# Two-layer mixture-of-experts encoder on one core: expert outputs added to the residual rows in DRAM

## The chip, the core and the metric

The kernel runs on one core of one Trainium2 chip. The metric is the device time of a run in microseconds; the kernel before takes 2674.23 us (median of 3 runs, 2671.6 to 2676.23). A core has TensorE (PE), VectorE (DVE), ScalarE (ACT), GpSimd (POOL) and SyncE (SP, which issues most transfers). They run beside each other and are ordered by semaphores only. Transfers issued by any of them run on the same 16 DMA engines. The profile is of one execution.

## What is computed

The input x is 1024 tokens of 1024 floats (f32). There are two layers, each a token mixer and then a mixture of experts (MoE), each with a norm before it and added to x:

```python
for i in range(2):
    if i == 0:
        x = x + short_conv_mixer(rms_norm(x, w), conv_w_in, conv_k, conv_w_out)
    else:
        x = x + mla_mixer(rms_norm(x, w), ...)        # latents 384+256+64, 8 heads, full softmax
    x = x + hier_moe(rms_norm(x, ffn_w), ...)

def hier_moe(h):                                      # 64 experts in 8 groups of 8
    g_sel = argmax(h @ w_group + b_group)             # one group per token
    e_top = top2(expert logits of that group + bias)  # two experts in it
    gate  = g_prob[g_sel] * e_prob[e_top] / sum(e_prob[e_top])
    out[token] += gate * ((silu(h @ w_gate[e]) * (h @ w_up[e])) @ w_down[e])   # w: 1024x384, 384x1024
```

Every expert's weights (4.7 MB) are read once per layer, 302 MB a layer. A token has two choices, so there are 2048 rows of 1024 floats of expert output in a layer.

## The kernel before

`build_trunk` runs four phases, one block each with a barrier of all engines behind it: `conv_phase` (mixer of layer 0 and its output projection), `moe_phase` of layer 0, `attention_phase` (latents, attention, output projection), `moe_phase` of layer 1. x lives in SBUF (`c.x`, 8 tiles of 128 tokens) throughout.

**Output projection** (`OutProjection`, L446 to L593, in both mixers). Per tile of tokens TensorE multiplies, VectorE adds to x (L538), ScalarE and GpSimd make the norm, and SP stores the normed rows to `h_rows` in DRAM (`sp_store_rows`, L471). The routing of two tiles at a time runs on VectorE (`dve_route`). At its end SP starts the first weights of the experts: gate and up weights have 4 slots, down weights 4 slots; two of the down slots lie in the arena, one in `c.turned` and its neighbours and one in a spare piece of the arena (L425 to L430).

**Expert layer** (`moe_phase`, L1025). VectorE ranks the choices of each expert (64 rows a round, one round here in each layer) and compares the ranks with columns (`find_ranks`, L1267, a one-hot of 128 x 2048); TensorE multiplies this with coded token numbers (`index_products`, L1392) into a table of DRAM row numbers, `gather_idx`, and VectorE makes `scatter_idx` beside it (L1346, L1347). A row of 1024 floats is handled as two half rows on 128 partitions. Then, for each expert, in an order written out by hand:

- GpSimd copies one column of the table (L1159), issues an indirect gather of the normed rows (L1162), later copies a column of the other table (L1169) and issues an indirect scatter of the outputs (L1172). Between them `complete` waits until the scatter of the expert before has landed, so at most one scatter is in flight.
- TensorE turns the gathered rows (L1410), multiplies gate and up (L1420), turns the products (L1430) and multiplies down (L1439). The order in one step is `gate_and_up(g)`, `turn_x(g+1)`, `down(g-1)`, `turn_h(g)`. After the first expert's `gate_and_up` and the second's `turn_x` it also does `index_products(r + 1)`.
- ScalarE copies products (L1210), makes SiLU (L1216) and copies the output (L1221). VectorE scales the turned rows (L1324) and multiplies (L1333).
- SP waits for each slot to be used and loads the next weights into it, the gate and up weights of expert g+4 after those of g, then the down weights, in that fixed order.

The scatters write to `y_rows`, 2 x 1024 rows: a row for the first choice of a token and one for the second, without the gates. Every row is written once.

**After the experts**, VectorE makes the gates (`make_gates`, L1297). In layer 0, VectorE and ScalarE split the weights of the latent projection, and SP loads pairs of rows from `y_rows` (L1010, six in this block, two later); in `attention_phase` VectorE adds both rows times their gates to each x tile (`combine`, L1813, two instructions a tile) before TensorE may turn it (L2001) and ScalarE may square it. In layer 1, SP loads the pairs (L1140), ScalarE scales the first row (L1247), VectorE adds the second and x (L1372, L1375), and SP stores x to the output (L1143).

**Attention**: 64 tiles (8 heads x 8 tiles of queries). TensorE makes 128 x 1024 scores in two halves of 512 (L2058, L2060), VectorE finds the row maximum of all 1024 (L1931) and minus the scaled maximum (L1934), ScalarE takes the exponential (L1743).

## Time and profile before

| | |
|---|---|
| median of 3 runs | 2674.23 us (2671.6 to 2676.23) |
| the profiled execution: device time | 2678.26 us |
| its span, first to last instruction | 2676.5 us |
| mean granted TensorE clock | 0.938 of full |
| PE / PEld / DVE / ACT / POOL busy | 87% / 55% / 30% / 24% / 25% |
| DRAM read / written | 687.59 MB / 46.14 MB |
| weight queue (q1) / GpSimd's queue (q0) | 666.65 MB / 33.64 MB |

The phases in the span: convolution mixer and projection from 0 to 412 us, experts of layer 0 to 1174 (their weights start at 399), latents to 1300, attention to 1759, projection to 1880, experts of layer 1 to 2642 (their weights start at 1867), the sum of pairs and the stores to the end. A busy share over the whole span mixes these. TensorE shows 87% although in the expert layers it is waiting for weights again and again; its granted clock there changes between its two levels.

### The profile page before, as it was taken

To read this page: it belongs to the slowest core of one execution; us is meant where nothing else is said; L and a number is where in the kernel's file an instruction comes from. 1 tells how busy PE (TensorE), PEld (TensorE's weight loads), DVE (VectorE), ACT (ScalarE), POOL (GpSimd) and SP (SyncE) were. 2 spreads that over 40 slices of the span, in tenths; PEclk is the share of its full clock that TensorE was granted. 3 is DMA by queue.
4 is the path that set the end of the run, shared out by engine and by line. 5 is a ranking of instruction groups with operands and counts; after the bars stand their busy time and mean duration, and the time that the engine had idled before them with its cause. 6 is when DMAs were issued, how large, how long until landed. Compare 5 with 4: busy or idle time off the path is not lost. (4 is left out here: it accounts for less than half of the span.)

```text
span 2676.5 us, 35898 instructions
## 1 busy us (share of the span) xinstructions
PE 2321.1 (87%) x12316; PEld 1463.0 (55%) x12318; DVE 809.3 (30%) x2022; ACT 636.9 (24%) x1360; POOL 679.6 (25%) x1092
## 2 busy tenths in 40 slices
PE   8999995988888888878799999999598888888883
PEld 6888782433333333348688898768243333333331
DVE  4322443100000000045578777644310000000003
ACT  4000221111110111134366666642011111111111
POOL 3222211212222212211655555211122122122120
PEclk9999997999999999989899999999799999999997
DMA  5111219999999999980000000101999999999997
GB/s 133 48 47 31 79 45 397 422 424 423 424 423 424 424 424 424 423 328 1 9 9 9 18 10 1 64 24 63 396 422 424 423 424 424 424 423 424 424 423 300
DMA packets 136774, 701.39 MB, mean 262 GB/s; under 512 B 36192, under 2 KB 65888, under 8 KB 87536
## 3 DMA queue, kind: packets, MB, share of 16 engines
q1 hardware_dynamic: 116208, 666.65, 60.7%
q0 software_dynamic: 20480, 33.64, 3.3%
q8 instruction: 49, 0.80, 0.1%
q14 instruction: 37, 0.30, 0.0%
HBM read 687.59 MB, written 46.14 MB: 274 GB/s over the span
## 5 line engine op out<-in xcount | busy, mean ns | idle before, releaser
L1420 PE MATMUL ps<-arena 128*64 128x384 f32 x2048 | 389.8, 539 | 90.1 <-DMA arena<-in_exp_w_up 88.0
L1420 PE MATMUL ps<-gate_up,arena 128*64 128x384 f32 x2048 | 384.9, 533 | 92.5 <-issue 92.5
L1324 DVE TENSOR_TENSOR arena<-ps,xw 128x512 f32<-128x512 f32 x128 | 88.6, 692 | 957.1 <-PE ps L1410 957.1
L1420 PEld LDWEIGHTS ps<-gate_up,arena 128*64 128x64 f32 x2048 | 181.3, 149 | 264.8 <-issue 183.9
L1420 PEld LDWEIGHTS ps<-arena 128*64 128x64 f32 x2048 | 158.5, 150 | 290.5 <-issue 242.2
L1210 ACT ACTIVATE arena<-ps 128x384 f32<-128x384 f32 x128 | 62.9, 491 | 898.7 <-PE ps L1420 898.7
L943 PE MATMUL ps<-hT_split,w_split 128*128 128x512 f32 x1152 | 265.6, 392 | 7.3 <-DVE hT_split L837 7.3
L1439 PE MATMUL ps<-arena 128*64 128x512 f32 x1152 | 268.3, 600 | 0.0
L1169 POOL COPY col_idx<-scatter_idx 128x1 int32 (+1 forms) x128 | 23.4, 183 | 920.2 <-ACT arena L1221 899.4
L943 PEld LDWEIGHTS ps<-hT_split,w_split 128*128 128x128 f32 x1152 | 217.3, 189 | 53.1 <-DVE hT_split L837 8.0
L1221 ACT ACTIVATE arena<-ps 128x512 f32<-128x512 f32 x128 | 76.4, 597 | 372.9 <-PE ps L1439 364.1
L1162 POOL DMA_INDIRECT arena<-h_rows,col_idx x128 | 135.2, 1057 | 114.6 <-POOL col_idx L1159 93.0
L1333 DVE TENSOR_TENSOR arena<-arena,ps 128x192 f32<-128x192 f32 x128 | 45.4, 354 | 387.7 <-ACT arena L1216 387.7
L1172 POOL DMA_INDIRECT y_rows<-arena,col_idx x128 | 132.0, 1031 | 112.8 <-POOL col_idx L1169 112.8
L1439 PEld LDWEIGHTS ps<-arena 128*64 128x64 f32 x1152 | 74.7, 136 | 121.4 <-issue 109.6
L1410 PEld LDWEIGHTS ps<-ident,arena 128*128 128x128 f32 x512 | 71.8, 209 | 101.8 <-issue 101.8
L2058 PE MATMUL ps<-k_split,q_split 128*128 128x512 f32 x384 | 115.0, 408 | 5.8 <-DVE k_split L1926 5.8
L1410 PE MATMUL ps<-ident,arena 128*128 128x128 f32 x512 | 96.5, 311 | 26.1 <-DMA arena<-h_rows,col_idx 26.1
L2082 PE MATMUL ps<-probsT,v_split 128*128 128x256 f32 x768 | 108.7, 292 | 5.6 <-DVE probsT L1940 5.6
L1430 PEld LDWEIGHTS ps<-ident,arena 128*128 128x128 f32 x384 | 53.6, 199 | 103.1 <-issue 102.2
L2082 PEld LDWEIGHTS ps<-probsT,v_split 128*128 128x128 f32 x768 | 101.4, 193 | 10.4 <-issue 6.6
L742 POOL TENSOR_TENSOR w_split<-arena,w_split 128x1024 fp32r<-128x1024 f32 x24 | 57.4, 2391 | 182.5 <-ACT w_split L779 182.5
(236 smaller groups left out, 3221.5 us busy)
## 6 DMA issues: line engine op xcount, KB each, us to landing
arena<-in_exp_w_down SPq DMA_DIRECT2D x96, 1536.0 KB, 28.6
arena<-in_exp_w_gate SPq DMA_DIRECT2D x64, 1536.0 KB
arena<-in_exp_w_up SPq DMA_DIRECT2D x64, 1536.0 KB
gate_up<-in_exp_w_gate SPq DMA_DIRECT2D x64, 1536.0 KB
gate_up<-in_exp_w_up SPq DMA_DIRECT2D x64, 1536.0 KB
down<-in_exp_w_down SPq DMA_DIRECT2D x32, 1536.0 KB, 28.6
arena<-in_conv_w_in SPq DMA_DIRECT2D x24, 512.0 KB, 3.8
arena<-y_rows SPq DMA_DIRECT2D x12, 1024.0 KB, 8.5
```

Of the source, the lines that this page charges most:

```text
L742: pool.tensor_tensor(w_split[:, j, LOW, :, :], w_raw[:, slot, :, :], w_split[:, j, HIGH, :, :], ALU.subtract).then_inc(w_low_ready, 1)
L943: last = pe.matmul(c.ps[:, 3 * h + j, :], w_split[:, j, a, k, :], hT_split[:, b, k, h * BANK:(h + 1) * BANK], start=(k == 0 and a == b), s ...
L1162: pool.indirect_dma_start(gathered[:, slot, :], None, h_halves, bass.IndirectOffsetOnAxis(ap=col_idx[:, slot, :], axis=0), bounds_check=2 ...
L1172: pool.indirect_dma_start(y_halves, bass.IndirectOffsetOnAxis(ap=col_idx[:, 2 + slot, :], axis=0), y[:, slot, :], None, bounds_check=4 * S ...
L1210: act.activation(gate_up[:, slot, :], c.ps[:, 2 + slot, 0:FF], ACT.Copy).then_inc(gate_up_copied, 1)
L1221: act.activation(y[:, slot, :], c.ps[:, 6 + slot, :], ACT.Copy).then_inc(y_copied, 1)
L1324: dve.tensor_tensor(xT[:, slot, :, :, :].rearrange("p j h m -> p (j h) m"), c.ps[:, slot, :].rearrange("p (a m) -> p a m", m=RANKS), bc(c. ...
L1410: last_ = pe.transpose(c.ps[:, slot, j * P:(j + 1) * P], rows[:, j, :], c.ident[:, :])
L1420: last_ = pe.matmul(c.ps[row:row + RANKS, 2 + slot, 0:FF], xT[:, slot, j, half, :], w_gate_up[w_slot][:, i, (4 * half + j) * FF:(4 * half ...
L1439: last_ = pe.matmul(c.ps[half * RANKS:(half + 1) * RANKS, 6 + slot, :], hidden[:, slot, j, :], w_down[w_slot][:, j, half * BANK:(half + 1) ...
L2058: pe.matmul(out, q_split[:, a, 0, q], k_split[:, h % 2, 2 * b, keys], start=(n == 0), stop=False)
L2082: last = pe.matmul(c.ps[:, 7, 0:2 * P], v_split[:, a, (q // 4 * NT + kt) % V_RING, :], probsT[:, b, kt, :], start=(kt == 0 and a == b), st ...
```

## The change

- The DRAM tensor `y_rows` (2048 rows) is gone, and so are `scatter_idx` and the ring of pair buffers. New is `x_rows` (1024 rows). During each output projection SP also stores every x tile, in layer 0 to `x_rows` and in layer 1 to the output tensor, each ahead of the normed rows of that tile.
- The scatters have `compute_op=ALU.add`: they add to the rows of `x_rows` or of the output. They use the same row numbers as the gathers.
- The gates are made at the begin of a round in the expert layer, ahead of the first expert's `expert_x`; they are split in three bf16 parts, multiplied with the choice (`gate_coded`) and spread by 48 matmuls (`spread_gates`) to one column for each expert. ScalarE's copy of an expert's output takes that column as its scale. `find_ranks(r + 1)` moves behind these.
- After layer 0, SP loads 8 x tiles of 512 KB from `x_rows` into `c.x`, and TensorE and ScalarE wait for them directly. After layer 1, nothing follows the last scatter.
- The third down slot lies in x tiles 5 to 7, whose rows are in DRAM by then; the one-hot and the gate pieces lie in x tiles 0 to 3.
- In the attention, the row maximum is found in two halves, each after its own half of the scores, and one instruction takes the larger and scales it.

```diff
@@ ExpertWeights
-        self.down.append(c.arena[:, self.SPARE_AT:self.SPARE_AT + KF * D].rearrange("p (j d) -> p j d", d=D))
+        self.down.append(c.x[:, NT - KF:, :])
@@ OutProjection
+    def sp_begin_sums(self, sp, t):
+        sp.wait_ge(self.x_added, 2 * t + 2)
+        sp.dma_start(self.sum_rows[t * P:(t + 1) * P, :], self.c.x[:, t, :]).then_inc(self.sums_begun, 16)
     def sp_store_rows(self, sp):
         for t in range(NT - 1):
+            self.sp_begin_sums(sp, t)
             self.norm.sp_store(sp, t)
         sp.wait_ge(self.products, 2 * NT)
         self.experts.load_gate_up(sp, 0, 0)
+        self.sp_begin_sums(sp, NT - 1)
         self.norm.sp_store(sp, NT - 1)
...
+        sp.wait_ge(self.sums_begun, 16 * NT)
@@ LatentPlaces
-    def load_y(self, sp, t):
-        src = self.c.y_rows.rearrange("(k t p) d -> t p k d", k=2, p=P)[t]
-        sp.dma_start(self.y_pair[t % Y_RING], src).then_inc(self.y_loaded[t % Y_RING], 16)
+    def load_x(self, sp, t):
+        sp.dma_start(self.c.x[:, t, :], self.c.x_rows[t * P:(t + 1) * P, :]).then_inc(self.x_loaded[t], 16)
@@ moe_phase, SP
                 sp.wait_ge(y_stored, count * NE + AHEAD)
-                for t in range(Y_RING):
-                    places.load_y(sp, t)
-            else:
-                sp.wait_ge(y_stored, count * NE + AHEAD)
                 for t in range(NT):
...
-                sp.wait_ge(stored, 16 * NT)
+                    places.load_x(sp, t)
@@ moe_phase, GpSimd
-                pool.tensor_copy(col_idx[:, 2 + slot, :], scatter_idx[:, bass.ds(e, 1)]).then_inc(pool_step, 1)
+                pool.tensor_copy(col_idx[:, 2 + slot, :], gather_idx[:, bass.ds(e, 1)]).then_inc(pool_step, 1)
...
-                pool.indirect_dma_start(y_halves, bass.IndirectOffsetOnAxis(ap=col_idx[:, 2 + slot, :], axis=0),
-                                        y[:, slot, :], None,
-                                        bounds_check=4 * S - 1, oob_is_err=False).then_inc(scatter_done[slot], 16)
+                to_rows = bass.IndirectOffsetOnAxis(ap=col_idx[:, 2 + slot, :], axis=0)
+                pool.indirect_dma_start(sum_halves, to_rows, y[:, slot, :], None, compute_op=ALU.add,
+                                        bounds_check=2 * S - 1, oob_is_err=False).then_inc(scatter_done[slot], 16)
@@ moe_phase, ScalarE
-                act.activation(y[:, slot, :], c.ps[:, 6 + slot, :], ACT.Copy).then_inc(y_copied, 1)
+                act.activation(y[:, slot, :], c.ps[:, 6 + slot, :], ACT.Copy,
+                               scale=gate_cols[:, bass.ds(e, 1)]).then_inc(y_copied, 1)
@@ moe_phase, VectorE
+            def code_gates(chain):
+                rest = gates[:, :, :]
+                for part in range(GATE_PARTS - 1):
+                    chain.sync(dve.tensor_copy(rounded[:, part, :, :], rest))
+                    chain.sync(dve.tensor_copy(gate_parts[:, part, :, :], rounded[:, part, :, :]))
+                    left = gate_rest if part == 0 else gate_parts[:, GATE_PARTS - 1, :, :]
+                    chain.sync(dve.tensor_tensor(left, rest, gate_parts[:, part, :, :], ALU.subtract))
+                    rest = left
+                for k in range(2):
+                    coded_k = dve.tensor_tensor(gate_coded[:, k, :, :, :], bc(chosen[:, k, :, :], 2, GATE_PARTS),
+                                                bc(gate_parts[:, :, k, :].rearrange("p a t -> p t a"), 3, NE), ALU.mult)
+                coded_k.then_inc(gates_coded, 1)
...
-                find_ranks(r + 1)
-                g0 = r * NE
-                expert_x(g0, 0)
+                g0 = r * NE
+                make_gates(in_round)
+                code_gates(in_round)
+                expert_x(g0, 0)
+                dve.wait_ge(gate_products, r + 1)
+                dve.tensor_copy(gate_cols, c.ps[:, IDX_BANK, FF + NE:FF + 2 * NE]).then_inc(gate_cols_ready, 1)
+                find_ranks(r + 1)
...
-            make_gates()
@@ moe_phase, TensorE
+            def spread_gates(r):
+                pe.wait_ge(gates_coded, r + 1)
+                for n in range(2 * NT):
+                    for part in range(GATE_PARTS):
+                        last_ = pe.matmul(c.ps[:, IDX_BANK, FF + NE:FF + 2 * NE], onehot[:, n, :],
+                                          gate_coded[:, n // NT, n % NT, part, :], start=(n + part == 0),
+                                          stop=(n == 2 * NT - 1 and part == GATE_PARTS - 1))
+                last_.then_inc(gate_products, 1)
...
                 pe.wait_ge(gate_up_copied, g0 + free(1))
+                spread_gates(r)
                 index_products(r + 1)
@@ attention_phase, VectorE
-            def combine(t):
...
             def find_max(s):
                 slot = s % 2
-                dve.wait_ge(scores, s + 1)
-                dve.tensor_reduce(row_max[:, slot, :], c.ps[:, 2 * slot:2 * slot + 2, :].rearrange("p a b -> p (a b)"),
-                                  X, ALU.max).then_inc(max_found, 1)
-                dve.wait_ge(max_found, s + 1)
-                dve.tensor_scalar(minus_max[:, slot, :], row_max[:, slot, :], -SCALE, None,
-                                  ALU.mult).then_inc(bias_ready, 1)
+                for half in range(2):
+                    dve.wait_ge(scores, 2 * s + half + 1)
+                    dve.tensor_reduce(row_max[:, slot, half:half + 1], c.ps[:, 2 * slot + half, :],
+                                      X, ALU.max).then_inc(max_found, 1)
+                dve.wait_ge(max_found, 2 * s + 2)
+                dve.tensor_scalar(minus_max[:, slot, :], row_max[:, slot, 0:1], row_max[:, slot, 1:2], -SCALE,
+                                  ALU.max, ALU.mult).then_inc(bias_ready, 1)
@@ attention_phase, TensorE
             def turn_x(t):
-                pe.wait_ge(x_added, t + 1)
+                pe.wait_ge(places.x_loaded[t], 16)
```

## Rows read from the trace of the kernel before

**Rows 1.** Busy time by stretch: us, PE, PEld, DVE, ACT, POOL busy, clock, DMA share, GB/s.
```profile
560.00:1080.00 520.00, 445.64 (x2256) 197.19 (x2254) 46.04 (x88) 58.53 (x132) 109.50 (x177) 0.93 1.01 424
1300.00:1700.00 400.00, 387.51 (x2441) 348.39 (x2440) 313.77 (x917) 250.44 (x590) 207.92 (x403) 1.00 0.03 10
...
2674.00:2676.00 2.00, 0.00 (x0) 0.00 (x0) 0.00 (x0) 0.00 (x0) 0.00 (x0) 0.50 0.05 18
```

**Rows 2.** Chain of waits, layer 1: start us, us, what.
```profile
2036.03 5.38 PE ps L1420 x32
...
2045.91 37.10 DMA arena<-in_exp_w_up
```

**Rows 3.** Timeline, end of layer 1: start us, us, engine, line, operation [idle before].
```profile
2635.11 0.98 POOL L1172 DMA_INDIRECT y_rows<-arena,col_idx  x1 [0.86 <-POOL col_idx L1169]
...
2638.35 0.18 POOL L1169 COPY col_idx<-scatter_idx 128x1 int32<-128x1 int32 x1 [2.25 <-ACT arena L1221]
...
2639.39 0.98 POOL L1172 DMA_INDIRECT y_rows<-arena,col_idx  x1 [0.86 <-POOL col_idx L1169]
2641.79 12.05 SPq L1140 DMA_DIRECT2D arena<-y_rows  x8
```

**Rows 4.** The scatters of layer 0, by tile: durations in ns, first and last start.
```profile
L1172 POOL DMA_INDIRECT y_rows<-arena,col_idx x64: 984/1032/1493, 459.7 to 1171.4; - x64
...
DMA to landing us min/median/max: 2.6/7.3/8.4
```

**Rows 5.** Timeline, end of layer 0 and begin of the latents.
```profile
1171.09 6.99 DVE L1020 SCALAR_TENSOR_TENSOR w_lat_low<-arena,norm_w,w_lat_high 128x704 fp32r<-128x704 f32 x8 [0.32 <-ACT w_lat_high L1014]
...
1174.65 0.90 SPq L1010 DMA_DIRECT2D arena<-y_rows  x2
...
1176.80 1.01 SPq L1010 DMA_DIRECT2D rows<-y_rows  x2
1179.20 0.38 SPq L1624 DMA_DIRECT2D arena<-in_mla_w_q_up  x1
...
1182.28 1.97 PE L2001 MATMUL ps<-ident,x 128*128 128x128 f32 x8 [12.72 <-DVE x L1813]
```

**Rows 6.** Timeline, first and last of the 19 steps of the gates, layer 1.
```profile
2634.43 0.22 DVE L1257 TENSOR_TENSOR arena<-exps,picked 128x64 f32<-128x64 f32 x1
...
2638.59 0.17 DVE L1257 TENSOR_TENSOR gates<-arena 128x8 f32<-128x8 f32 x1
```

**Rows 7.** Timeline, begin of the experts of layer 1.
```profile
1893.09 2.29 DVE L1268 TENSOR_TENSOR onehot<-arena,rank_of_col 128x2048 bf16<-128x2048 f32 x1
1893.33 2.10 POOL L1159 COPY col_idx<-gather_idx 128x1 int32<-128x1 int32 x1 [10.28 <-DVE scatter_idx L1347]
...
1904.76 1.12 PE L1410 MATMUL ps<-ident,arena 128*128 128x128 f32 x4 [13.10 <-DMA arena<-h_rows,col_idx]
...
1915.08 1.10 PE L1396 MATMUL ps<-coded,onehot 128*128 128x64 bf16 x32
...
1916.50 0.61 PE L1430 MATMUL ps<-ident,arena 128*128 128x128 f32 x3 [0.33 <-ACT arena L1210]
...
1925.87 0.33 SPq L443 DMA_DIRECT2D arena<-in_exp_w_down  x1
```

**Rows 8.** Busy time by stretch, two microseconds at the begin of layer 1.
```profile
1924.00:1926.00 2.00, 2.00 (x12) 0.62 (x9) 0.00 (x0) 0.05 (x1) 0.00 (x0) 1.00 0.25 104
```

**Rows 9.** DMA queues from 560 to 1080 us: packets, MB, share; issues with their number.
```profile
q1 hardware_dynamic: 19125, 208.93, 95.3%
q0 software_dynamic: 7101, 11.35, 5.8%
...
arena<-h_rows,col_idx POOLq DMA_INDIRECT x45
```

**Rows 10.** GpSimd's waits from 560 to 1080 us: total us, times, longest.
```profile
POOL col_idx L1169 <- ACT arena L1221: 330.7, 44, 9.6
```

**Rows 11.** The maximum over all scores of a tile, by line: duration in ns, times.
```profile
L1931 DVE TENSOR_REDUCE turned<-ps x64: 1224/1225/1226, 1317.1 to 1747.2; 128x1 f32<-128x1024 f32 x64
```

More of the change, by code:

```diff
@@ L989, in __init__ @@
         self.low_ready = sems("w_lat_low_ready")
-        self.y_loaded = [sems(f"y_pair_loaded{i}") for i in range(Y_RING)]
+        self.x_loaded = [sems(f"x_sums_loaded{t}") for t in range(NT)]
         self.small_loaded = sems("latent_small_loaded")
@@ L1082, in moe_phase @@
     y_copied = sems("y_copied")
-    y_pair_loaded = [sems(f"y_pair_loaded{i}") for i in range(Y_RING)]
-    gates_ready = sems("gates_ready")
-    first_scaled = sems("first_scaled")
-    summed = sems("summed")
-    x_added = sems("x_added")
-    stored = sems("stored")
+    gates_coded = sems("gates_coded")
+    gate_products = sems("gate_products")
+    gate_cols_ready = sems("gate_cols_ready")
     def done(g):
@@ L1100, in moe_phase @@
     h_halves = c.h_rows.rearrange("t (h d) -> (t h) d", h=2)
-    y_halves = c.y_rows.rearrange("t (h d) -> (t h) d", h=2)
+    sum_halves = (c.out[0] if last else c.x_rows).rearrange("t (h d) -> (t h) d", h=2)
     def rounds(eng):
@@ L1242, in _ @@
                 return
-            act.wait_ge(gates_ready, 1)
-            for t in range(NT):
-                act.wait_ge(y_pair_loaded[t % Y_RING], 16 * (t // Y_RING + 1))
-                first = y_pair[:, t % Y_RING, 0, :]
-                act.activation(first, first, ACT.Copy, scale=gates[:, 0, t:t + 1]).then_inc(first_scaled, 1)
         @block.vector
@@ L1295, in _, with make_gates, tt, red @@
             dve.tensor_copy(n_rounds[:, :], t_[0][:, 1:2]).then_inc(rounds_ready, 1)
-            def make_gates():
+            def make_gates(chain):
+                def tt(out, a, b, op):
+                    chain.sync(dve.tensor_tensor(out, a, b, op))
+                def red(out, a, op):
+                    chain.sync(dve.tensor_reduce(out, a, X, op))
                 group, first, second = (c.picked[:, i, :, :] for i in range(3))
@@ L1306, in make_gates @@
                     red(t_[4], e, ALU.add)
-                    step.sync(dve.reciprocal(t_[5 + i], t_[4]))
+                    chain.sync(dve.reciprocal(t_[5 + i], t_[4]))
                 for i, total in enumerate((5, 6, 6)):
@@ L1310, in make_gates @@
                 tt(t_[10], t_[8], t_[9], ALU.add)
-                step.sync(dve.reciprocal(t_[11], t_[10]))
+                chain.sync(dve.reciprocal(t_[11], t_[10]))
                 for k in range(2):
@@ L1632, in _ @@
             load_router(sp, c, 1, router_loaded)
-            for t in range(Y_RING, NT):
-                sp.wait_ge(x_squares, t - Y_RING + 1)
-                places.load_y(sp, t)
             with sp.Fori(1, NH // 2) as pair:
@@ L1640, in _ @@
             sp.wait_ge(up_products, TILES)
-            sp.wait_ge(scores, TILES - NT)
+            sp.wait_ge(scores, 2 * (TILES - NT))
             out_projection.sp_load(sp)
@@ L1807, in sine_inputs @@
                 dve.tensor_scalar(turns_, turns_, PI_MAX, -PI_MAX, ALU.min, ALU.max).then_inc(sin_in, 1)
-            def combine(t):
-                dve.wait_ge(places.y_loaded[t % Y_RING], 16 * (t // Y_RING + 1))
-                for k in range(2):
-                    wait(dve, pair_added, t + 1 if k == 1 else 0)
-                    dve.scalar_tensor_tensor(out=c.x[:, t, :], in0=places.y_pair[t % Y_RING][:, k, :],
-                                             scalar=c.gates[:, k, t:t + 1], in1=c.x[:, t, :], op0=ALU.mult,
-                                             op1=ALU.add).then_inc((pair_added, x_added)[k], 1)
             def low_x(t):
@@ L2061, in score @@
                                          start=False, stop=(a == LOW))
-                last.then_inc(scores, 1)
+                    last.then_inc(scores, 1)
             def turn_probs(s, turned):
```

88 lines of the change are left out of this document (34 added, 54 removed).

## The prediction

> **What bounds the kernel now.** I read the 40 slices of the page first, then the busy time by stretch, the chain of waits, the DMA queues, and the timelines of the places that the diff touches. The two expert layers are bounded by the transfer of their weights: over 520 us in the first of them the DMA engines are full at 424 GB/s while VectorE, ScalarE and GpSimd are busy 46, 59 and 110 us [rows 1]. The chain of waits shows it too: one expert's products at 2036.03, then 37.1 us of waiting for weights until 2083.0, and so on [rows 2]. In these layers a microsecond of engine work costs nothing and a microsecond of transfer costs a microsecond. The attention stage is bounded by TensorE, busy 387.5 of 400 us with VectorE at 313.8 [rows 1].
>
> **Part 1, the end of layer 1: gain.** Now the last scatter starts at 2639.39 and has landed when SP issues the pair loads at 2641.79 [rows 3]. After that 8.4 MB of pairs are read and combined and 4.2 MB stored, until DMA's share falls to 0.05 in the stretch from 2674 to 2676 [rows 1]; the span ends at 2676.5. All of this goes: the output is complete when the last scatter has landed. The last transfer ends near 2674.2 (the small share in those 2 us is some 0.1 us, and a write receipt), so I keep 2.3 us from it to the end of the span; the end would be 2641.8 + 2.3 = 2644.1, a gain of 32.4 us. Against it: an adding scatter must read its destination before it writes, and the trace of before has no adding transfer. An unloaded scatter of before takes 2.4 us from its start to SP's next step [rows 3]; one more trip costs between 0 and another 2.4. I take 1.0, below the middle because the 2.4 hold 0.98 us of the issuing instruction. The scatter before the last starts at 2635.11 and would land at 2638.4, just as the last one's index copy starts anyway (2638.35) [rows 3]; with 2.4 more it would delay that by 1.5. Gain: 31.4 us (28.5 to 32.4).
>
> **Part 2, the end of layer 0.** Now SP issues six pair loads from 1174.65 to 1177.81, VectorE splits the weights until 1178.08, the stage's barrier lets SP begin the next stage at 1179.20, and two VectorE additions to the first tile hold TensorE until 1182.28 [rows 5]. From there the latent projection is one unbroken run of matmuls, so the later pairs and additions are hidden now and taking them out gives nothing: only the first start counts. In the changed kernel the last scatter lands 1.0 later, at 1175.65; SP issues eight loads at 0.53 us (3.16 us for six), until 1179.9; with the same 1.4 us to the barrier's end and 0.2 to the first transpose TensorE begins at 1181.5, its rows long there. The wait that takes the additions' place is SP's eight issues ahead of the barrier. Gain: 0.8 us (2.6 at best, a loss of 1.5 with 2.4 more in the landing).
>
> **Part 3, the begin of both expert layers: loss.** The gates, their three bf16 parts and two products with the choice move ahead of the first expert on VectorE. The 19 small steps of the gates take 4.33 us (2634.43 to 2638.76) [rows 6]; the 6 of the coding at the same 0.23 us make 1.4; the two products of 1,536 elements are priced from the 2,048-element comparison of 2.29 us [rows 7] at 1.7 each. Together 9.2 us, from 1893.1 to 1902.3. The cover is the first gather, whose rows are turned at 1904.76 to 1905.9 [rows 7]: this costs nothing, with 3.6 us to spare. What is moved too is that comparison (L1268). GpSimd's first index copy, 0.18 us elsewhere [rows 3], stood 2.10 us beside it and ended with it (1895.43 and 1895.38) [rows 7]. Without it the first gather starts up to 1.9 us earlier, I take 1.8, and with it the first expert; the spare is then 1.8 us.
>
> The Trainium skill says ("SBUF — State Buffer", section "Who interferes with whom") that a VectorE instruction with two SBUF inputs keeps GpSimd from reading SBUF while it runs. By that rule, the trace agrees with its 2.10 us, the gate steps that now stand there may hold the copy for one of them, 0.2 us, and no more.
>
> Behind the first expert's products TensorE now gets: 48 products that spread the gates (32 index products take 1.10 us from 1915.08 [rows 7], so 1.65, until 1916.73), then it waits for VectorE's copy (0.2, with the hand-over 0.4) and the comparison (2.29), until 1919.5; then the 32 index products, and the turn of the first hidden rows starts at 1920.8 instead of 1916.50 [rows 7]. That is 4.3 us later; the second expert's multiply, queued behind the comparison on VectorE, fits in. Net of the 1.8 it is 2.5 us. Nothing covers it: the DMA engines have by then filled every slot and stand at a share of 0.25 [rows 8] until the first down products release the next load at 1925.87 [rows 7], and transfer bounds the layer from there. So 5.0 us for both layers (0 if TensorE's wait is half as long, 9 if the early gather brings nothing). The x stores in each output projection (4.2 MB) run where DMA idles; the last of them (0.5 MB, 1.2 us), pushed in among the first weights, ends in the same hole: 0, or 1.2 each if the hole closes.
>
> **Part 4, the adding scatters in the transfer-bound stretch: the large loss.** In the same 520 us, 45 gathers and the scatters (44 by [rows 10]) took 5.8%, 30.2 us, or 0.339 us of all 16 engines each; the weight queue moved 208.93 MB in 95.3%, at 422 GB/s [rows 9]. The two queues fill the time together, so a scatter's bytes displace weights one for one. An adding scatter reads its source and its destination and writes once. The low end: the second read runs beside other writing and costs 0. The nearest row for the other end: a whole further scatter, 0.339 us. The 2,048 choices of a layer make 8.4 MB of rows; 123 of the 128 scatters lie in the bound stretches, 16.1 MB, and at the stream's 422 GB/s their second read takes 38.3 us (0.31 each; by 0.339 it is 41.7). I take 38.3, since gathers, scatters and loads share one budget in the rows whichever way they go.
>
> The Trainium skill ("Collectives: The Full Stack", section "The bandwidth ceiling: the fold count and why AG ≠ RS ≠ AR") puts a reduction inside the DMA engine at half a copy's rate, because it reads two sources and not because of the addition. By that rule the price is the one taken here; no run of this case shows it yet.
>
> Each scatter also waits on GpSimd for the earlier one to land, ahead of its index copy. Now GpSimd idles 330.7/44 = 7.5 us before that copy, and for ScalarE's result, not for the scatter [rows 10]; the median landing is 7.3 us [rows 4].
>
> **Part 5, attention.** The maximum of 1,024 elements takes 1.225 us, 64 times [rows 11]. Two halves cost about 0.16 us more and the first runs beside the second half's scores; but VectorE has 20% to spare and TensorE 3% [rows 1]. I take 1.0 us of gain from the last tiles, where TensorE waits a little (bounds: gain 4, loss 2).
>
> **Sum**, on the profiled execution's own 2678.3 us (span 2676.5): -31.4 - 0.8 + 5.0 + 38.3 - 1.0 = +10.1, so 2688.4. The median of the runs, 2674.2, is 4.1 lower; on it the forecast is 2684, slower by 0.4%. A measurement of this kernel tells about 0.2%, 5.3 us, from no change.
>
> **Rivals.**
> 1. The second read is hidden, the kernel is faster. The engines' writing side would be the bound, with reads from DRAM beside it. For it: no row separates the two sides. Against: DMA is as full whichever direction is under way. Part 4 falls to between 0 and 15 us; with 8, 2674.2 - 31.4 - 0.8 + 5.0 - 1.0 + 8 = 2654 (2646 to 2661).
> 2. The chain of scatters becomes the bound, the kernel is much slower. In layer 0 scatters start every 11.3 us (459.7 to 1171.4, 63 steps) [rows 4], 11.6 with part 4; copy and gap ahead of a start are 1.06 us [rows 3]. So it decides from a landing of 10.6 us. A loaded landing is 7.3, an unloaded 2.6 [rows 4]: if the queueing of 4.7 doubles with the second read, it is 12.0, the period 13.1, and 126 x (13.1 - 11.3) = 227 us replace part 4: 2873. For it: the queueing is there. Against: if only bytes are added, landing stays near 8.
> 3. The engine's addition is slow as well: 0.7 us a scatter instead of 0.31, 123 x 0.39 = 48 us more, 2732.
> 4. That the change doesn't do what it says, a result still stored at the end: the diff removes loads and stores there, so I give this nothing.
>
> **How the numbers follow.** The forecast 48% (its own range 2668 to 2702), rival 1 30%, rival 2 12%, rival 3 10%. The range, 2648 to 2735, leaves out the best end of rival 1 and nearly all of rival 2. Faster: rival 1 and the low end of the forecast's case, 0.32. Within 0.2%: 0.10. Slower: 0.58.
>
> **What would show it.** Four experts in the bound stretch take 47.1 us now (2083.1 less 2036.0 [rows 2]) and should take 48.3; at 47.1 rival 1 holds. The software queue's share should rise from 5.8% to about 8.5%. GpSimd should still wait for ScalarE before a scatter; if it waits for the landing, rival 2. DMA's hole behind the first four experts' weights should be 2.5 us longer in each layer, and the span should end some 5 us after the last scatter's start. I am wrong if four experts take the same time, or over 50 us.

## The result, and the profile after

The changed kernel takes 2682.8 us (median of 7 runs, 2678.8 to 2685.7) where the kernel before takes 2675.0 in runs beside it: 1.0027 times as long (1.0016 to 1.0039), slower by 0.3%. A second set of runs gave 1.0038 (1.0025 to 1.0052; its medians are 7.0 us apart). The forecast was 2684.

The profiled execution took 2681.45 us, its span is 2679.7, at a mean granted clock of 0.944. That is only 3.2 more than the profiled execution of before, which lay 3 us above its own median. The traces therefore show where 3.2 us come from; the other 4 to 5 between the medians lie in no single place that a trace shows.

The expert layers first. Busy time of the same stretches as [rows 1] and [rows 8], columns as there:

```profile
560.00:1080.00 520.00, 440.11 (x2238) 191.48 (x2236) 46.02 (x88) 61.59 (x132) 135.76 (x179) 0.94 1.02 414
1300.00:1700.00 400.00, 382.23 (x2394) 345.33 (x2395) 320.95 (x972) 243.39 (x584) 212.76 (x413) 0.99 0.03 10
```

The DMA engines are as full as before, and move 414 GB/s where it was 424. VectorE has 7 us more in the attention stage (the halves of the row maximum). The queues, issues and GpSimd's waits in that first stretch, against [rows 9] and [rows 10]:

```profile
q1 hardware_dynamic: 18664, 203.85, 92.5%
q0 software_dynamic: 9978, 11.59, 9.3%
...
x_rows<-arena,col_idx POOLq DMA_INDIRECT x45, 9.6
arena<-h_rows,col_idx POOLq DMA_INDIRECT x44, 9.5
```
```profile
POOL col_idx L1163 <- DMA x_rows<-arena,col_idx: 192.6, 30, 6.9
POOL col_idx L1163 <- ACT arena L1215: 117.6, 15, 8.6
```

GpSimd's queue is counted with about as many bytes as before (11.59 MB, where it was 11.35) and takes 9.3% of the engines instead of 5.8%. It has 2,877 packets more, some 64 for each of the 45 scatters: in the trace's packet records an adding scatter goes in packets of 2 KB, 176 ns each, where before gathers and scatters go in packets of 4 KB, 160 ns each. A read of the destination shows in no byte count. In 30 of 45 cases GpSimd waits for the landing of the scatter before, where it waited for ScalarE 44 times of 44. The scatters themselves, by tile, against [rows 4]: the issuing instruction takes 1.60 us instead of 1.03 and the landing, here over both layers, 9.6 instead of 7.3.

```profile
L1167 POOL DMA_INDIRECT x_rows<-arena,col_idx x64: 1566/1602/2202, 461.8 to 1192.3; - x64
```
```profile
DMA to landing us min/median/max: 3.7/9.6/10.5
```

The chain of waits in layer 1, against [rows 2]. Its early part runs from scatter to scatter. Its late part runs from weights to weights, four experts in 48.2 us (2486.74 to 2534.97) instead of 47.1:

```profile
2000.30 9.40 DMA out<-arena,col_idx
2010.12 0.17 POOL col_idx L1163
...
2486.74 5.38 PE ps L1427 x32
2496.63 38.22 DMA arena<-in_exp_w_up
2534.97 5.38 PE ps L1427 x32
```

The timeline at the end of layer 1, against [rows 3]. The index copy of the last scatter now waits 3.23 us for a landing, and the span ends at 2679.7, 8.4 us after the last scatter's start (37.1 before). Of these 8.4 us the landing takes 3.7:

```profile
2665.14 2.79 PE L1446 MATMUL ps<-down,arena 128*64 128x512 f32 x12 [1.15 <-DVE arena L1343]
...
2665.48 1.57 POOL L1167 DMA_INDIRECT out<-arena,col_idx  x1 [0.86 <-POOL col_idx L1163]
...
2670.28 0.18 POOL L1163 COPY col_idx<-gather_idx 128x1 int32<-128x1 int32 x1 [3.23 <-DMA out<-arena,col_idx]
2671.32 1.57 POOL L1167 DMA_INDIRECT out<-arena,col_idx  x1 [0.86 <-POOL col_idx L1163]
```

Most of the other 4.7 is a drain, GpSimd's last instruction of the block but for semaphores, from 2675.6 on. Its two executions (minimum, median and maximum in ns), one at the end of each expert layer, here and in the kernel whose scatters do not add (plain_scatter below):

```profile
L1112 POOLq DRAIN  x2: 2918/2987/3056, 1198.0 to 2675.6; - x2
```
```profile
L1112 POOLq DRAIN  x2: 1535/1604/1672, 1175.8 to 2636.0; - x2
```

The beginning of the experts of layer 0 (that of layer 1 has the same order), against [rows 7]:

```profile
445.30 1.56 PE L1403 MATMUL ps<-gate_coded,onehot 128*128 128x64 bf16 x48
...
446.90 0.22 DVE L1363 COPY x<-ps 128x64 f32<-128x64 f32 x1 [9.51 <-PE ps L1403]
447.04 2.28 DVE L1259 TENSOR_TENSOR onehot<-arena,rank_of_col 128x2048 bf16<-128x2048 f32 x1
...
449.38 1.11 PE L1394 MATMUL ps<-coded,onehot 128*128 128x64 bf16 x32 [2.52 <-DVE onehot L1259]
450.32 0.58 PE L1437 MATMUL ps<-ident,arena 128*128 128x128 f32 x3
...
459.66 0.33 SPq L442 DMA_DIRECT2D arena<-in_exp_w_down  x1
```

From the starts of such marks the span can be cut into pieces that add up. "Again" is a second profile of the same kernel, taken for the experiments.

| piece, us | before | after | changed by |
|---|---|---|---|
| begin to first scatter of layer 0 | 459.7 | 461.8 | +2.1 |
| first to last scatter of layer 0 | 711.7 | 730.5 (again 731.3) | +18.8 |
| last scatter to first turn of x | 10.9 | 10.5 | -0.4 |
| first turn to first score | 130.2 (again 128.5) | 126.2 (again 124.3) | -4.0 |
| first to last score | 433.8 | 430.7 (again 432.6) | -3.1 |
| to the barrier before layer 1 | 135.8 | 136.6 (again 134.3) | +0.8 |
| barrier to first scatter of layer 1 | 45.7 | 47.1 (again 47.7) | +1.4 |
| first to last scatter of layer 1 | 711.6 | 727.9 (again 728.6) | +16.3 |
| last scatter to the end | 37.1 | 8.4 (again 8.4) | -28.7 |
| sum | 2676.5 | 2679.7 | +3.2 |

### The profile page after: what moved, and what is told of

Its sections match the earlier page's. It is cut to its first block and busy times, and to the rows that moved or that the text cites. A ratio compares the mean times of both kernels' runs of the same rounds, so it can differ in the third digit from the quotient of the medians.

```text
span 2679.7 us, 36367 instructions
## 1 busy us (share of the span) xinstructions
PE 2321.2 (87%) x12412; PEld 1456.8 (54%) x12414; DVE 790.8 (30%) x2070; ACT 635.3 (24%) x1352; POOL 748.9 (28%) x1092
## 5 line engine op out<-in xcount | busy, mean ns | idle before, releaser
L1427 PE MATMUL ps<-arena 128*64 128x384 f32 x2048 | 380.8, 529 | 74.6 <-DMA arena<-in_exp_w_up 72.4
L1427 PEld LDWEIGHTS ps<-gate_up,arena 128*64 128x64 f32 x2048 | 173.0, 147 | 258.1 <-issue 199.6
L1427 PEld LDWEIGHTS ps<-arena 128*64 128x64 f32 x2048 | 154.8, 148 | 268.8 <-issue 223.3
L1163 POOL COPY col_idx<-gather_idx 128x1 int32 (+1 forms) x128 | 23.2, 181 | 888.1 <-ACT arena L1215 343.9
L1215 ACT ACTIVATE arena<-ps,x 128x512 f32<-128x512 f32 x128 | 88.0, 688 | 456.8 <-PE ps L1446 453.8
L1446 PE MATMUL ps<-arena 128*64 128x512 f32 x768 | 188.6, 628 | 0.0
L1167 POOL DMA_INDIRECT x_rows<-arena,col_idx x64 | 103.1, 1610 | 56.2 <-POOL col_idx L1163 56.2
L1167 POOL DMA_INDIRECT out<-arena,col_idx x64 | 102.5, 1602 | 57.8 <-POOL col_idx L1163 57.8
```

Source lines behind the costliest of these rows:

```text
L1167: pool.indirect_dma_start(sum_halves, to_rows, y[:, slot, :], None, compute_op=ALU.add, bounds_check=2 * S - 1, oob_is_err=False).then_inc ...
L1215: act.activation(y[:, slot, :], c.ps[:, 6 + slot, :], ACT.Copy, scale=gate_cols[:, bass.ds(e, 1)]).then_inc(y_copied, 1)
L1427: last_ = pe.matmul(c.ps[row:row + RANKS, 2 + slot, 0:FF], xT[:, slot, j, half, :], w_gate_up[w_slot][:, i, (4 * half + j) * FF:(4 * half ...
L1446: last_ = pe.matmul(c.ps[half * RANKS:(half + 1) * RANKS, 6 + slot, :], hidden[:, slot, j, :], w_down[w_slot][:, j, half * BANK:(half + 1) ...
```

## The experiments

The disputed thing was part 4: the trace after agrees with the second read (more engine time, 414 GB/s) and in part with rival 2 (waits for landings). Three kernels take these apart.

**Scatters without the addition.**

```diff
-                pool.indirect_dma_start(sum_halves, to_rows, y[:, slot, :], None, compute_op=ALU.add,
+                pool.indirect_dma_start(sum_halves, to_rows, y[:, slot, :], None,
```

> The changed kernel with scatters that write and do not add: the additions to x and of the second choice are left out, so the output is not the layer's. Theory A (the destination's read takes 0.26 us of all 16 engines for each scatter): 31 to 32 us less over both layers, and some 2 us less at each end from the shorter landing: 2647 where the changed kernel is 2683 (2642 to 2651); the weight stretch is back at 423 GB/s and four experts take 47.1 us. Rival B (the longer chain of landings costs it): the same time here, so plain_slow_chain decides. Rival C (a part of the loss is from the gate column in ScalarE's copy or from x in the arena's place): 2655 or more.

Measured: 2639.8 us beside 2678.6 for before, ratio 0.9856 (0.9836 to 0.9875); against the changed kernel's 1.0027 that is 46 us less (43 between the medians themselves), more than the 36 expected. The same stretch of 560 to 1080 us:

```profile
560.00:1080.00 520.00, 445.59 (x2266) 197.03 (x2264) 46.00 (x88) 61.48 (x132) 108.32 (x178) 0.94 1.01 424
```
```profile
q1 hardware_dynamic: 19132, 209.04, 95.3%
q0 software_dynamic: 7040, 11.21, 5.7%
```

These are the rows of before again. From first to last scatter it is 711.8 and 711.1 us, so the whole loss inside the layers hangs on the addition; the gate columns, the scale in ScalarE's copy and the moved tiles cost nothing there. The span is 41.0 us shorter than the changed kernel's: 18.8 + 16.8 in the layers, 2.7 at the end (5.7 instead of 8.4, of which the landing is 1.3 and the drain 1.4), 2.3 at the first turn of x (8.2 instead of 10.5), and small pieces. Rival C falls. I had counted each end at 2 and the layers at 32. Unloaded, at the end of layer 1, a plain scatter lands in 2.4 us, the least of all:

```profile
DMA to landing us min/median/max: 2.4/7.3/8.6
```

**The chain of landings made longer, without a byte.**

```diff
                         complete(g0 + e - 4, slot)
+                        for i, words in enumerate((D, D // 4)):
+                            pool.memset(c.x[:, 4, 0:words], 0.0).then_inc(slow_step, 1)
+                            pool.wait_ge(slow_step, 2 * (g0 + e - 4) + i + 1)
+                            pool.sem_inc(slow_seen, 1)
```

> As plain_scatter (the additions left out), with two fills of 1024 and 256 words on GpSimd between the landing of a scatter and the next index copy: the chain from scatter to scatter is about 2.8 us longer, near the 11.1 us of the adding one, without a byte more in DRAM traffic. Theory A (bytes, not the chain): within 3 us of plain_scatter, 2650, and 423 GB/s. Rival B (the chain costs): most of the 32 us come back, 2670 to 2680, with the DMA engines under 1.0.

Measured: 2640.3 us, ratio 0.9862 (0.9842 to 0.9882), the same as plain_scatter. Ahead of the fills GpSimd now waits for the landing, 45 times of 45 (in plain_scatter it waited for ScalarE, 44 times of 44); behind them it still waits for ScalarE 26 times, so in 19 of 45 cases the longer chain came last. The engines stay at 424 GB/s:

```profile
POOL x L1190 <- DMA x_rows<-arena,col_idx: 195.4, 45, 5.2
POOL col_idx L1164 <- ACT arena L1220: 67.1, 26, 3.9
```
```profile
560.00:1080.00 520.00, 446.32 (x2262) 197.17 (x2260) 45.99 (x88) 61.49 (x132) 166.58 (x269) 0.93 1.01 424
```

The early steps of the layer went from 9.2 to some 10.4 us (not quite the adding kernel's 11.1) and layer 0 took 711.5 us from first to last scatter. A longer chain shows in the waits, and even stands in the chain of waits of the changed kernel, and costs nothing: it only slows how fast the first experts use up weights that are already there, while the DMA engines go on filling. Rival B falls for chains up to this length; the last 0.7 us, up to the adding kernel's 11.1, are early_copy's below.

**A whole further scatter.**

```diff
...
                                         bounds_check=2 * S - 1, oob_is_err=False).then_inc(scatter_done[slot], 16)
+                pool.indirect_dma_start(spare_halves, to_rows, y[:, slot, :], None,
+                                        bounds_check=2 * S - 1, oob_is_err=False).then_inc(scatter_done[slot], 16)
```

> As plain_scatter (the additions left out), with each scatter issued a second time to a DRAM tensor that nothing reads: what one whole further scatter of 64 KB displaces. Theory A (a scatter displaces 0.34 us of weights, and the destination's read of an adding one is a part of that): 123 x 0.34 = 42 us over plain_scatter, 2689. Rival (the read of the destination costs as much as a read and a write together): 123 x 0.26 = 32 us, 2679. If the landing of both becomes the bound (steps over 12 us with the engines under 1.0) it is more.

A scatter moves 128 KB on average, and not 64: 64 half rows of 2 KB.

Measured: 2693.5 us, ratio 1.0056 (1.0041 to 1.0071), 53.7 over plain_scatter beside it. The queues from 560 to 1080 us:

```profile
q1 hardware_dynamic: 18575, 202.92, 92.5%
q0 software_dynamic: 10580, 17.20, 8.7%
```

First to last scatter is 734.1 and 733.7 us, 22.3 and 22.6 more than in plain_scatter. The last step of a layer, where nothing is transfer-bound, is 1.5 and 1.0 of that (5.8 and 5.3 us against 4.4), so the 62 steps before it give 20.8 and 21.6, 0.34 us a scatter: what the prediction read from before's share. The ends are 6.2 and 5.0 us longer (11.9 instead of 5.7, 13.2 instead of 8.2); 5.2 of the 6.2 is GpSimd's drain, 6.84 us instead of 1.67. Small pieces take back some 3. The rows also show that share is a poor price for an adding scatter: the queue takes 9.3% of the engines with adding scatters and 8.7% with twice as many plain ones, yet the adding ones displace less. The sum of the two queues' shares is 101.8% with additions and 101.2% here. Taken together, the three kernels show that the addition costs DMA engine time and not waiting. Whether this time is the read of the destination or goes with the packets of half the size, no run separates.

**The chain shorter by the index copy.**

```diff
+                pool.tensor_copy(col_idx[:, 2 + slot, :], gather_idx[:, bass.ds(e, 1)]).then_inc(pool_step, 1)
+                if landed is not None:
+                    complete(landed, 1 - slot)
                 pool.wait_ge(y_copied, g + done(0))
-                pool.sem_inc(scatters_begun, 1)
-                pool.tensor_copy(col_idx[:, 2 + slot, :], gather_idx[:, bass.ds(e, 1)]).then_inc(pool_step, 1)
...
```

> The changed kernel with GpSimd's index copy for a scatter ahead of the wait for the earlier scatter's landing: the chain from scatter to scatter loses the copy and its hand-over, 1.04 us. Theory A (in the expert layers bytes are the bound, the chain that stands at 11.1 us through the first 25 experts costs nothing since the DMA engines are full all the same): only the two ends gain, 1.0 us each: 2681 where the changed kernel is 2683; the steps through the first 25 experts become 10.1 us and 414 GB/s stays. Rival B (the chain of landings sets the time of these experts): up to 25 x 1.04 in each layer, 2631 to 2650.

Measured: 2681.8 us, ratio 1.0021 (1.0011 to 1.0032). Theory A's size, within the noise of nothing; B's 30 to 50 us are not there. The early steps fell only from 11.1 to 10.7 us, since a landing takes 9.6 and the issue 1. The mean of the first 25 steps did not fall at all (11.27 and 11.17 us in the two layers, in the changed kernel 11.27 and 11.17): what the shorter chain gives at first, the wait for weights takes back. So the chain does not set these experts' time in the adding kernel either.

**The next round's comparison behind the last expert.**

```diff
+                sp.wait_ge(idx_products, count + 1)
...
-                find_ranks(r + 1)
...
                 with dve.Fori(0, NE // 2 - 1) as pair:
...
                 expert_h(g0 + NE - 1, 1)
+                find_ranks(r + 1)
...
                 spread_gates(r)
-                index_products(r + 1)
...
                 down(g0 + NE - 1, 1, DOWN_SLOTS - 1)
+                index_products(r + 1)
```

> The changed kernel with the next round's comparison and its 32 index products behind the last expert instead of behind the first. Theory (they hold the turn of the first hidden rows and nothing covers that): the turn starts right behind the 48 products that spread the gates, 3.4 us earlier in each layer, the DMA hole closes by as much, 6.8 us less: 2676 where the changed kernel is 2683. The comparison at the end lies beside the last scatters. Rival (the hole is set by the first gather and the scatters' chain, not by the turn): less than 2 us.

(The first line makes SP's loads of x wait for these products too; the first turn of x does not move by it, 10.6 us behind the last scatter instead of 10.5.)

Measured: 2682.3 us, ratio 1.0022 (1.0012 to 1.0032), so not 6.8 less: by the changed kernel's two ratios 1 to 4. The timeline did what was meant, the first turn starts 3.7 us earlier and the first load behind the hole 2.7:

```profile
446.64 0.61 PE L1438 MATMUL ps<-ident,arena 128*128 128x128 f32 x3
...
456.96 0.33 SPq L442 DMA_DIRECT2D arena<-in_exp_w_down  x1
```

The hole of DMA closes: 455 to 470 us, first the changed kernel, then this one.

```profile
455.00:470.00 15.00, 15.00 (x82) 6.33 (x80) 1.74 (x3) 2.79 (x6) 3.11 (x4) 1.00 0.83 324
```
```profile
455.00:470.00 15.00, 15.00 (x86) 6.38 (x84) 1.40 (x3) 2.30 (x5) 3.29 (x5) 1.00 0.99 397
```

0.16 of 15 us is 2.4 us; what comes earlier than that finds the engines full. This much does arrive: from the barrier to the 63rd scatter of a layer it is 768.7 and 767.6 us, against 771.4 and 769.1 in the changed kernel (773.5 and 770.3 in its second profile). The last step then gives most of it back. It takes 7.5 us in both layers instead of 5.9 and 5.8, because the comparison now lies beside the issue of the scatter before the last, which takes 3.05 us instead of 1.57:

```profile
1182.82 2.28 DVE L1260 TENSOR_TENSOR onehot<-arena,rank_of_col 128x2048 bf16<-128x2048 f32 x1
...
1183.50 3.05 POOL L1168 DMA_INDIRECT x_rows<-arena,col_idx  x1 [0.84 <-POOL col_idx L1164]
```

My expectation named this place and gave it no price, and took the shift of an instruction for the gain.

**The halves of the row maximum alone, in the kernel before.**

```diff
-                dve.wait_ge(scores, s + 1)
-                dve.tensor_reduce(row_max[:, slot, :], c.ps[:, 2 * slot:2 * slot + 2, :].rearrange("p a b -> p (a b)"),
+                for half in range(2):
+                    dve.wait_ge(scores, 2 * s + half + 1)
+                    dve.tensor_reduce(row_max[:, slot, half:half + 1], c.ps[:, 2 * slot + half, :],
...
```

> The kernel before with only the row maximum in two halves. Between the first score and the last turn of the probabilities the changed kernel took 436.2 us against 439.7, and 0.8 of that went again at a lower clock behind it; a head takes 55.93 us instead of 56.03 and each of the last pairs of tiles 10.68 instead of 11.15. Theory (the halves alone do this): 2.7 to 3.5 us less than before, 2672 where before is 2675. Rival (the gain comes from the combining that left VectorE, or from the clock): no change, the head stays at 56.03. In both, the 4.4 us that the changed kernel gained behind the latent projection, where TensorE's clock rose two steps of 6.6 us earlier, are not expected here: if they appear, they are chance or come from the later phase of the stage.

Measured: 2672.8 us beside 2676.0, ratio 0.9982 (0.9974 to 0.9991), 2.4 to 7 us less. In its trace the scores take 430.7 us from first to last, as in the changed kernel (433.8 before). The gain is the halves' own.

**The additions of layer 0's pairs cut short, in the kernel before.**

```diff
-                    dve.scalar_tensor_tensor(out=c.x[:, t, :], in0=places.y_pair[t % Y_RING][:, k, :],
+                    dve.scalar_tensor_tensor(out=c.x[:, t, 0:8], in0=places.y_pair[t % Y_RING][:, k, 0:8],
...
```

> The kernel before with the additions of layer 0's pairs to x cut to 8 of 1024 columns (the rest of the addition is left out, so the output is not the layer's); loads, waits and order stay. Theory (my part 2: only the first start counts): the first turn comes two long additions earlier, about 2 us, and nothing else in the stage changes: 2673 where before is 2675. Rival (VectorE's additions beside the latent projection are what keeps TensorE's clock down for longer at the steps behind it, or the later additions hold TensorE too): 6 to 10 us less, with the clock high from the third step.

Measured: 2671.3 us, ratio 0.9981 (0.9971 to 0.9990), 5 us less: between the two. In its trace the first turn comes 2.0 us earlier behind the last scatter (8.9 instead of 10.9), as my part 2 says, and the clock rose in the third of the steps. And **the kernel before once more**, for its profile:

> The kernel before once more, for its profile. Seven steps of TensorE follow one another between the latent projection and the first scores, 6.6 us each at a granted clock of 0.5 and 4.36 us at 1.0. In the profile of before and in halves the clock rose after the fifth, in best after the fourth; in hybrid, which has the same layer 0, after the second, as in all profiles with the changed layer 0 except the changed kernel's own (third). Theory (chance in either form): this time may differ from the first by 2.2 us for every step, in either direction. Rival (the old layer 0 makes it late): again the fourth or fifth.

Measured: span 2676.0, the clock high after the third step. These steps explain why the time from the first turn to the first score differs. Here they are in the trace of before (turns of queries and keys between the latent projection and the first score, TensorE), with the busy time and the granted clock (third number from the end) of a stretch:

```profile
1284.49 1.09 PE L2045 MATMUL ps<-ident,rows 128*128 128x128 f32 x4 [1.89 <-issue]
1291.10 1.09 PE L2045 MATMUL ps<-ident,rows 128*128 128x128 f32 x4 [1.89 <-issue]
1297.71 1.09 PE L2045 MATMUL ps<-ident,rows 128*128 128x128 f32 x4 [1.89 <-issue]
1303.44 0.63 PE L2045 MATMUL ps<-ident,rows 128*128 128x128 f32 x4 [1.90 <-issue]
1307.80 0.63 PE L2045 MATMUL ps<-ident,rows 128*128 128x128 f32 x4 [1.89 <-DVE rows L1909]
```
```profile
1281.00:1300.00 19.00, 13.32 (x41) 10.71 (x41) 7.84 (x33) 3.34 (x15) 11.23 (x22) 0.50 0.00 0
```

and in the hybrid below, whose layer 0 and latent stage are those of before:

```profile
1281.22 0.66 PE L2514 MATMUL ps<-ident,rows 128*128 128x128 f32 x4 [1.88 <-DVE rows L2377]
1285.61 0.63 PE L2514 MATMUL ps<-ident,rows 128*128 128x128 f32 x4 [1.89 <-DVE rows L2377]
1289.97 0.63 PE L2514 MATMUL ps<-ident,rows 128*128 128x128 f32 x4 [1.89 <-DVE rows L2377]
```
```profile
1280.00:1290.00 10.00, 5.00 (x29) 4.15 (x30) 6.28 (x29) 2.71 (x12) 8.07 (x15) 1.00 0.00 1
```

A step takes 6.6 us at the low level of the clock (0.50) and 4.36 at the high one (1.00). The seven steps took 39.6, 39.6, 38.6, 36.4, 35.1 and 32.8 us in six traces with the old layer 0, and 35.1, 33.7 and five times 32.8 in seven with the new one. The last rise to the high level came in the first to the fifth of the seven steps: in the fifth in before, and in the first in the hybrid, where the expectation says the second. All else from the first turn to the first score took 90.5 to 92.1 in both kinds: so the additions behind the first tile were hidden, as part 2 said, and what differs is when the clock rises. The means are 37.0 and 33.3. Chance has its part (hybrid and best differ by 5.8 with the same code), but the new kind never took more than 35.1. What it is in the old layer 0 that holds the clock down longer is open; cutting the additions short did not settle it.

**Each form where it pays: layer 0 as before, layer 1 with adding scatters, halves.**

```diff
+        spare = c.arena[:, self.SPARE_AT:self.SPARE_AT + KF * D].rearrange("p (j d) -> p j d", d=D)
+        self.down.append(spare if layer == 0 else c.x[:, NT - KF:, :])
...
         moe_phase(c, 0, experts[0], places)
         attention_phase(c, experts[1], places)
-        moe_phase(c, 1, experts[1])
+        moe_phase_sums(c, 1, experts[1])
```

> Layer 0 as before (pairs of rows from y_rows, gates behind the experts), layer 1 as changed (adding scatters to the output), row maximum in halves. Theory (each layer's price stays its own): the sum of layer 1's terms, +0.5 at the projection, +1.2 at the begin, +15.0 for 62 adding scatters, -27.2 at the end, is -10.5; with -2.7 for the halves -13: 2662 where before is 2675 (2656 to 2668). Rival (a good part of the loss in layer 0 is not from the additions and stays, or the gain at the end shrinks with it): 2668 or more.

Measured: 2662.6 us beside 2676.0, ratio 0.9957 (0.9944 to 0.9970). It beats both. Its scatters take 728.6 us in layer 1 and its span ends 8.4 after the last. With late ranks and the early copy in layer 1 added:

> The hybrid (layer 0 as before, layer 1 with adding scatters, halves) with late ranks and the early index copy in layer 1. Theory (the terms add): the hybrid's 2662 less 3.4 for the ranks and 1.0 for the last copy: 2658 where before is 2675. Rival (the ranks are covered in this place): 2661.

Measured: 2665.5 us beside 2678.6, ratio 0.9946 (0.9930 to 0.9962): not to be told from the hybrid. Here too the comparison lies beside the issue of the scatter before the last, 3.31 us instead of 1.56, and the last step of layer 1 takes 7.6 us instead of 6.3.

**The changed kernel once more**, its pieces in the table above:

> The changed kernel once more beside fresh runs of the kernel before: the ratio should be 1.0027 within its interval (1.0016 to 1.0039), its layers' scatters from first to last 18 to 19 us longer than before's 711.7, and from the last scatter to the end of the span 8.4 us.

Measured: 2682.5 us beside 2675.5, ratio 1.0038 (1.0025 to 1.0052). The layers came out at 731.3 and 728.6, 19.6 and 17.0 more than before's, where 18 to 19 was said.

## Why the prediction was right

The main mechanism held: adding scatters take DMA engine time, and in the transfer-bound stretches this displaces weights for longer than the end of layer 1 gains. That the forecast of 2684 met the median of 2682.8 so closely is luck in part. The terms as the traces give them add up to +3.6 us (-27.2 + 1.1 - 4.0 + 4.1 + 32.7 - 3.1), where the forecast had +10.1 and the profiled executions differ by 3.2; the medians are 7 to 8 us apart, and no term explains the 3 to 5 us between.

- **Part 1, the end of layer 1.** Forecast -31.4, measured -28.7 from the last scatter to the end and +1.5 for the last step (5.8 instead of 4.3 us): -27.2. The second trip was sized about right. The last adding scatter landed in 3.7 us where a plain one took 2.4, and the one before it in 4.5 where a plain one took 2.7: 1.3 and 1.8 more, where I took 1.0 with a bound of 2.4. The mis-sized term is the 2.3 us that I kept from the last transfer to the end of the span. Behind the landing it is 4.7 us here and 3.3 in plain_scatter, with GpSimd's drain of 3.06 and 1.67 us in it. In before the same drain took 1.67 us and lay beside the loads of the pairs, so it cost nothing. The delay of the last scatter by 1.5 was named as the low end, and came.
- **Part 2, the end of layer 0.** Forecast -0.8; -0.4 behind the last scatter, which itself comes 1.5 late: +1.1, inside the bounds. The last landing of layer 0 took 5.5 us where it took 3.2. That later additions were hidden is borne out by the constant 91 us. What I did not see is the clock behind the latent projection, worth -4.0 in this pair of traces.
- **Part 3, the beginnings.** Forecast +5.0. What counts is the time from the barrier to the first load behind DMA's hole (459.66 in the rows above): 45.7 us in the mean of thirteen such beginnings with the new order (44.4 to 48.1), 44.0 in ten with the old one (43.7 to 44.2). That is 1.8 a layer instead of 2.5, and in the changed kernel's own first profile 0.6 and 1.1. The new order's beginnings spread by more than their mean cost; why is open. The first gather started 2.0 us earlier (12.3 instead of 14.3 us behind the barrier), 1.8 forecast. The spread took 1.56 (1.65 forecast), the comparison 2.28 (2.29). The x stores are new ahead of the barrier of layer 0. It came at 414.99 in the first profile and 413.08 in the second; the mean of seven traces with them is 414.1 and of six without 413.5. If the stores are the cause, which no run takes apart, they cost some 0.5 us in the mean, where I had put nothing: +4.1 in all.
- **Part 4, the second read.** Forecast +38.3, 0.31 us a scatter. From the first to the 63rd scatter, so without the last step, which part 1 has, the layers with adding scatters take 724.5 (mean of four, layer 0) and 723.0 us (mean of six, layer 1), before 707.5 and 707.3. These 17.0 and 15.7 are 32.7 us, or 0.26 us a scatter. (Other traces with the old layer 0 take up to 709.0, which would make it 0.25.) The size was inside the bounds of 0 to 0.34; rival 1, with no price or 8 us, fell, and so did rival 3, with 0.7. That it is the read of the destination that costs this is argued, not shown.
- **The rule on reductions.** An adding scatter takes 0.34 + 0.26 = 0.60 us of the engines where a plain one takes 0.34. The Trainium skill ("Collectives: The Full Stack", section "The bandwidth ceiling: the fold count and why AG ≠ RS ≠ AR") puts a reduction at half a copy's rate; the runs give 0.57.
- **Rival 2.** The landing rose to 9.6, under the 10.6 from which I let it decide. Yet the chain of waits does go from scatter to scatter through the first 25 experts of a layer, at some 11.1 us a step. My point was placed by the mean step of the layer (11.3), but before, the first eight steps ran at 9.2 and the bound ones at 11.7. In the early part the point is passed, and costs nothing, as plain_slow_chain and early_copy show; the condition of this rival should have been the steps of the bound part.
- **Part 5, attention.** Forecast -1.0 (bounds -4 to +2), measured -3.1 in the trace, and 2.4 to 7 us alone. Both parts of it are in the steps: each head 55.93 instead of 56.03 us, each of the last pairs of tiles 10.68 instead of 11.15.
- **What would show it.** Four experts took 48.2 (48.3 said). The queue's share rose to 9.3% (8.5 said), because engine time of an adding scatter is not its displaced time. GpSimd waits for the landing 30 times of 45, which I had made the sign of rival 2: wrong sign. DMA's hole was to be 2.5 us longer in each layer; in layer 0 the DMA share from 455 to 470 us is 0.83 and 0.70 in the two profiles, against 0.86 and 0.84 in those of before, so some 0.5 and 2.1 us. The span ends 8.4 us after the last scatter, not 5 (5.7 by the prediction's own terms).

## What to carry to other kernels

Count the transfers of both forms against what bounds the stage they stand in: adding in DRAM saves a load, a sum and a store where they stand bare at the end, and costs more DMA engine time where the engines are full. Here it lost in layer 0, whose loads were hidden anyway, and won 10 us in layer 1 (by the table's last four pieces), so the better kernel does it once. A wait on a chain, even one in the chain of waits, costs only if the resource that bounds the stage falls idle; read its share there before pricing it. Work that is moved out of one uncovered place must be priced where it lands: the comparison lost at the end most of what it had gained at the beginning.

## What the runs showed of the hardware

- An adding indirect scatter with 128 row numbers, 64 of them valid on average (2 KB each): instruction 1.60 us on GpSimd (1.03 plain), landing 9.6 us loaded (7.3), 3.7 to 4.5 us unloaded (2.4 to 2.7), 9.3% of the engines with the gathers (5.7%), 0.26 us of weights displaced beyond the 0.34 of a plain one. It goes in packets of 2 KB at 176 ns, where a plain one's 4 KB take 160 ns; the byte counts do not show a read of the destination.
- GpSimd's drain at the end of the block, behind the last landing: 2.92 to 3.06 us with adding scatters (six traces), 1.53 to 1.68 with plain ones, 6.84 with two plain ones in each step.
- The index copy of the next gather, right behind a scatter's issue on GpSimd, took 0.73 us behind an adding one and 0.20 behind a plain one (medians of 127). Beside VectorE's comparison of 2048 elements the issue of an adding scatter took 3.05 us instead of 1.57.
- TensorE's granted clock went from 0.50 to 1.00 for the rest of the same seven light steps in the first to the fifth of them, and differed in executions of the same code too (32.8 us for the seven in hybrid, 38.6 in best). Over all traces that alone moved the span by up to 6.8 us (39.6 against 32.8), more than this kernel's 0.2%.
